# One rotary query product for two heads of a decoder step on one core

## What is computed

```python
z = x @ p['w_in'] + p['b_in']            # x: (tokens, 1024)
q = (_rms_norm(z_q, p['q_norm_g']) @ p['w_uq']).reshape(B, T, N_HEADS, QK_NOPE + QK_ROPE)   # 8 heads, 128 + 64
q_nope = q[..., :QK_NOPE]
q_rope = _apply_rope(q[..., QK_NOPE:], cos[:, None, :], sin[:, None, :])
c_kv = _rms_norm(z_kv, p['kv_norm_g'])
k_rope = _apply_rope(z_kr, cos, sin)     # one rotary key for all heads
...
def _apply_rope(x, cos, sin):
    x1, x2 = jnp.split(x, 2, axis=-1)
    return jnp.concatenate([x1 * cos - x2 * sin, x1 * sin + x2 * cos], axis=-1)
```

## Time and profile before

| | us |
|---|---|
| runs shown | 2083.44, 2084.58, 2088.0 |
| median | 2084.58 |
| profiled execution | 2083.54 |
| its span | 2081.7 |
| TensorE busy in it | 2027.8 |
| VectorE busy | 1268.9 |
| ScalarE busy | 651.7 |
| GpSimd busy | 566.2 |

### The profile page before, as it was taken

One profiled execution on the slowest core, in us unless ns is written; L12 is line 12 of the kernel. 1 busy time (PEld: TensorE's weight loads), 2 busy tenths in 40 slices (PEclk: granted clock), 3 DMA queues, 4 the chain that ended last, 5 costly groups with the idle time before them and its releaser, 6 DMA issues.

```text
span 2081.7 us, 34162 instructions
## 1 busy us (share of the span) xinstructions
PE 2027.8 (97%) x13468; PEld 1923.1 (92%) x13468; DVE 1268.9 (61%) x1746; ACT 651.7 (31%) x1099; POOL 566.2 (27%) x284
## 2 busy tenths in 40 slices
PE   8999999999999999989999999999999999999998
PEld 8999999998988888876669999999999999999997
DVE  2999999946647677655344325754545454454547
ACT  4222222225234454444342113422222222222222
POOL 4812443302110010124311245322222222222224
PEclk9999999999999999999999999999999999999999
DMA  6422233216410001145644332111111111111113
GB/s 199 158 94 76 85 105 101 80 52 213 136 58 20 16 13 43 36 166 229 242 178 145 121 113 82 31 51 51 41 51 41 51 41 51 41 51 41 51 31 128
DMA packets 164042, 182.92 MB, mean 88 GB/s; under 512 B 19917, under 2 KB 136927, under 8 KB 159821
## 3 DMA queue, kind: packets, MB, share of 16 engines
q1 hardware_dynamic: 146144, 108.68, 17.3%
q0 software_dynamic: 8320, 46.27, 5.8%
q10 hardware_dynamic: 9469, 26.36, 3.3%
HBM read 150.21 MB, written 31.93 MB: 87 GB/s over the span
## 4 chain that ended last, share of the span: by engine, by line
PE 87%; DVE 7%; issue 3%; ACT 3%; ACTq 0%; DMA 0%; POOL 0%; DVEq 0%; SPq 0%
PE psb L2124 27%; PE psa L2124 27%; PE psb L2763 6%; PE psa L2763 6%; PE psb L2313 4%; PE psa L2313 4%; PE psb L2564 1%; PE pst L2543 1%; DVE ptl L1712 1%; PE psa L2511 1%; PE psb L2511 1%; DVE nmx L1696 1%; PE pst L2386 1%; PE pst L2546 1%; PE psb L2266 1%
## 5 line engine op out<-in xcount | busy, mean ns | idle before, releaser
L1434 POOL TENSOR_TENSOR wlo<-wraw,whi 128x1024 fp32r<-128x1024 f32 x64 | 173.2, 2720 | 560.8 <-ACT whi L1226 560.8
L1536 DVE SCALAR_TENSOR_TENSOR pst<-g_ext,wtap,pst 128x512 f32<-128x512 f32 x464 | 306.9, 748 | 0.0
L1304 POOL TENSOR_TENSOR wlo<-wraw,whi 128x1024 fp32r<-128x1024 f32 x64 | 155.2, 2431 | 385.1 <-ACT whi L749 288.4
L2014 DVE TENSOR_SCALAR hg<-ueg,fwv,vec 128x1024 f32<-128x1024 f32 x22 | 20.4, 925 | 231.3 <-ACT ueg L1260 226.9
L2124 PE MATMUL psa<-x1h,whi 128*128 128x352 f32 x504 | 109.1, 324 | 0.0
L2124 PE MATMUL psb<-x1h,whi 128*128 128x352 f32 x504 | 109.0, 324 | 0.0
L2124 PE MATMUL psa<-x1h,wlo 128*128 128x352 f32 x504 | 108.6, 323 | 0.0
L2124 PE MATMUL psb<-x1h,wlo 128*128 128x352 f32 x504 | 108.6, 323 | 0.0
L2124 PE MATMUL psa<-x1l,whi 128*128 128x352 f32 x504 | 108.5, 323 | 0.0
L2124 PE MATMUL psb<-x1l,whi 128*128 128x352 f32 x504 | 108.5, 323 | 0.0
L2017 DVE SCALAR_TENSOR_TENSOR hg<-ueg,fwv,hg 128x1024 f32<-128x1024 f32 x44 | 96.9, 2203 | 5.7 <-DVE hg L2014 0.2
(11 more groups left out here) (540 smaller groups left out, 5290.5 us busy)
## 6 DMA issues: line engine op xcount, KB each, us to landing
wraw<-in_w_up SPq DMA_DIRECT2D x44, 512.0 KB, 3.7
wraw<-in_w_in SPq DMA_DIRECT2D x37, 512.0 KB, 3.8
wraw<-in_w_down SPq DMA_DIRECT2D x22, 512.0 KB, 3.6
xt_d<-tmp POOLq DMA_DIRECT2D x8, 528.0 KB, 3.4
gb_d<-stg ACTq DMA_DIRECT2D x8, 528.0 KB, 2.6
ga_d<-stg ACTq DMA_DIRECT2D x8, 528.0 KB, 3.6
ma_d<-stg ACTq DMA_DIRECT2D x8, 528.0 KB, 2.9
tmp<-gb_d SPq DMA_DIRECT2D x8, 528.0 KB, 3.8
```

The costliest lines, as they stand in the source:

```text
L1304: nc.gpsimd.tensor_tensor(wlo[:, n % HL, :], wraw[:, n % RAW, :], whi[:, n % HL, :].bitcast(F32), ALU.subtract).then_inc(lo_done, 1)
L1434: nc.gpsimd.tensor_tensor(wlo[:, (ns + 2) % HL, :], wraw[:, (ns + 2) % RAW, :], whi[:, (ns + 2) % HL, :].bitcast(F32), ALU.subtract).then_ ...
L1536: half[x] = link(nc.vector.scalar_tensor_tensor(out=dst, in0=src, scalar=tap(k_), in1=pst[:, x, :], op0=ALU.mult, op1=ALU.add))
```

## The change

1. **One rotary product for two heads.** The 128 weight columns of `pe_rope` now hold the 64 rotary columns of head 2i and the 64 of head 2i + 1, none of them swapped. It runs only at the end of odd heads (and once ahead of head 0). The loads shrink from three pieces for each head to two for each pair.
2. **Rotation out of PSUM.** For the even head VectorE reads psa crosswise: two products of 32 partitions with the halves exchanged and one of 64 (L1708, L1710 of the new code), then adds as before. The odd head's 64 partitions are copied by ScalarE in three instructions (64, 32 and 32 partitions) into a new buffer `qrb`, plain and with halves exchanged (`act_second_rope`). VectorE rotates them at the start of the even head: two products and an addition from SBUF to SBUF, around the first row maximum (`dve_second_rope`). `qrb` lies where `wukp` was loaded early, so that load now waits until the last rotation is done (`qr_t`).
3. **Even heads' ends reordered.** TensorE: key, `pe_prob` 6, `pe_out` 2, thirds 0 and 1 of the query, `pe_prob` 7, the last third, `pe_out` 3. ScalarE and VectorE follow.
4. **`pe_out` 2 and 3** start when the first group of `ptl` is made and wait for the second only at k = 4.
5. **The start.** x tiles rotate over pst, psb and two banks of psa. The first weight block is loaded second. Ten 128-column products of `ones` run ahead of the first transpose. The first third's products follow tiles 3 and 4, the second third's tiles 6 and 7.
6. **TensorE's three loops** are written out.

```diff
-        x_parts = lambda t: (psx[1][:, 0:2, :] if t % 2 else pst[:, :, :]).rearrange("p b (k n) -> p (b k) n", n=P)
+        WARM = 10
+        def x_parts(t):
+            if t == 8:
+                return psx[1][:, 2, 0:MT * NS].rearrange("p (k n) -> p k n", n=NS)
+            return (pst[:, :, :], psx[1][:, 0:2, :], psx[0][:, 1:3, :])[t % 3].rearrange("p b (k n) -> p (b k) n", n=P)
...
-                if t == 3:
+                if t == 1:
                     load(0, w_in_v[:, :, 0:P])
...
-                    for c, w, f in kr_parts:
-                        sp.dma_start(s0[:, 3:6, c:c + w], uq[:, :, bass.ds(2 * i * HQ + (s * HQ + DN + f), w)]).then_inc(hq_in, 16)
+                    if s == 0:
+                        for e in range(2):
+                            sp.dma_start(s0[:, 3:6, e * DR:(e + 1) * DR], uq[:, :, bass.ds(2 * i * HQ + (e * HQ + DN), DR)]
+                                         ).then_inc(hq_in, 16)
...
+            def act_second_rope(h):
+                act.wait_ge(proj_done, 2 * h + 1)
+                for to, p0, n in ((0, DR, DR), (DR, DR + 32, 32), (DR + 32, DR, 32)):
+                    ins = nc.scalar.activation(split(qrb[to:to + n, :]), psx[0][p0:p0 + n, :, 0:CH], ACT.Copy, scale=SCALE)
+                ins.then_inc(free[0], 2)
...
+            def dve_second_rope(h, part_):
+                if part_ == 0:
+                    dve.wait_ge(free[0], 6 * h + (U2[0] - 3))
+                    dve.wait_ge(qr_lo, h)
+                    nc.vector.tensor_tensor(qrf[0:DR, :], qrb[DR:P, :], cs[DR:P, :], ALU.mult)
+                    nc.vector.tensor_tensor(qrb[0:DR, :], qrb[0:DR, :], cs[0:DR, :], ALU.mult).then_inc(qr_t, 1)
+                else:
+                    dve.wait_ge(qr_t, 3 * h + 1)
+                    nc.vector.tensor_tensor(qrf[0:DR, :], qrf[0:DR, :], qrb[0:DR, :], ALU.add).then_inc(qr_t, 1)
+                    dve.wait_ge(qr_t, 3 * h + 2)
+                    sample_rope(h)
...
                     dve.wait_ge(proj_done, 2 * h + 1)
+                    for to, p0, t0, n in ((0, 32, DR, 32), (32, 0, DR + 32, 32)):
+                        nc.vector.scalar_tensor_tensor(out=split(qrt[to:to + n, :]), in0=psx[0][p0:p0 + n, :, 0:CH],
+                                                       scalar=SCALE, in1=split(cs[t0:t0 + n, :]), op0=ALU.mult, op1=ALU.mult)
...
                 for i in range(8):
+                    if s == 0 and i <= 1:
+                        dve_second_rope(h + 1, i)
                     dve_max(h, i)
...
+            pe.wait_ge(ones_set, 1)
+            for _ in range(WARM):
+                nc.tensor.matmul(psx[0][:, 0, 0:P], ones[:, :], ones[:, :], start=True, stop=True)
             pe.wait_ge(c_in, 16)
...
-                if t == 6:
+                if t == 3:
                     pe.wait_ge(lo_done, RAW + 1)
                     pe.wait_ge(free[0], x_tile_done(2))
                     first_third(0, range(0, 4))
+                if t == 4:
+                    first_third(0, range(4, KT))
+                if t == 6:
+                    pe.wait_ge(free[1], x_tile_done(5))
+                    pe.wait_ge(free[0], x_tile_done(4))
+                    first_third(1, range(0, 4))
                 if t == 7:
-                    first_third(0, range(4, KT))
...
             def pe_out(h, s, i2, a_):
-                pe.wait_ge(pt_lo, 12 * h + (cum(2 * a_ + 2) + 2))
+                pe.wait_ge(pt_lo, 12 * h + (cum(2 * a_ + 2) + (2 if a_ < 2 else 1)))
...
+                    if k == 4:
+                        pe.wait_ge(pt_lo, 12 * h + (cum(2 * a_ + 2) + 2))
...
+                if more and s == 0:
+                    pe_key(h + 1, 1)
+                    pe_prob(h, 6)
+                    pe_out(h, s, i2, 2)
+                    pe_query(h + 1, 1, h, (0, 1))
+                    pe_prob(h, 7)
+                    pe_query(h + 1, 1, h, (2,))
+                    pe_out(h, s, i2, 3)
+                    return
...
-            with pe.Fori(1, H // 2 - 1) as i:
+            for i in range(1, H // 2 - 1):
```

More of the change, by code:

```diff
@@ L1053, in act_head @@
                             hi_head_v(h + 1)
-                act_out(h, 2)
-                act_prob(h, 6)
-                if more:
-                    act_project(h + 1, 1 - s, "rope")
-                    act_project(h + 1, 1 - s, "query")
-                act_prob(h, 7)
-                if more:
-                    act_project(h + 1, 1 - s, "key")
-                else:
+                if more and s:
+                    act_second_rope(h + 1)
+                    act_out(h, 2)
+                    act_prob(h, 6)
+                    act_project(h + 1, 0, "rope")
+                    act_project(h + 1, 0, "query")
+                    act_prob(h, 7)
+                    act_project(h + 1, 0, "key")
+                elif more:
+                    act_project(h + 1, 1, "rope")
+                    act_project(h + 1, 1, "key")
+                    act_prob(h, 6)
+                    act_out(h, 2)
+                    act_prob(h, 7)
+                    act_project(h + 1, 1, "query")
+                else:
+                    act_out(h, 2)
+                    act_prob(h, 6)
+                    act_prob(h, 7)
                     for r in range(4):
@@ L2224, in _ @@
             last.then_inc(cl_p, 1)
-            with pe.Fori(CSUM, MT) as m:
+            for m in range(CSUM, MT):
                 in_products(m, 1)
@@ L2344, in pe_key @@
                                                  for k in range(2)])
-                last.then_inc(w_used, 1 + s)
+                last.then_inc(proj_done if s else w_used, 1 + s)
             def pe_values(h, i2, r):
@@ L2434, in pe_head @@
                 if more:
[L2435 removed]
+                    pe_query(h + 1, 0, h)
                 else:
@@ L2592, in _ @@
             pe_sample(0, 0, 0, first=True)
-            with pe.Fori(0, NB // 2 - 1) as i:
+            for i in range(0, NB // 2 - 1):
                 pe_sample(2 * i + 1, 1, i)
```

110 lines of the change are left out of this document (65 added, 45 removed).

## The result

The changed kernel takes 2069.38 us (median of 4 runs, 2067.01 to 2071.06), the kernel before 2085.56 with one more run (4 runs, 2083.44 to 2088.0). The ratio is 0.9922, 95% interval 0.991 to 0.9935. The forecast was 2070.0, between 2064.0 and 2077.5, so the time came out where it was expected. The profiled execution took 2068.43 us (span 2066.6), 15.11 less than the 2083.54 of before; 14.6 had been forecast between the two. The medians differ by more, 16.2 us, since the fourth run of the kernel before raised its median by 1.0.

The account below looks back on a forecast made before the run. TensorE was taken to bound the kernel, busy 2027.8 of 2081.7 us. Terms 17.4 + 2.0 - 1.3 - 2.0 - 1.5 + 0.5 - 0.5 gave 14.6 us gained, so 2070.0, range 2064 to 2077.5 for eight in ten.

Parts of the forecast that it names:

- even ends: Ends of even heads without the rotary product, reordered: 14.2 us instead of 18.55, four times 4.35, 17.4 gained.
- first group ahead of `pe_out`: Value products starting on the first group: 0.9 at three odd ends, 0.5 and 0.6 in head 7, 2.0 gained.
- third product ahead of head 0: VectorE's rotation out of PSUM has three products instead of two, uncovered ahead of head 0: 1.3 us lost.
- start of head 0: TensorE's wait for the first exponential grows by VectorE's two added products, 1.9, with `vl` 2.0 us lost.
- starts of heads 2, 4, 6: VectorE's 4.1 us of added rotation work mostly hidden; third value part waits 0.5, three times, 1.5 us lost.
- start: Start of the kernel up to the tables: reached at 31.9 to 33.0 instead of 33.19, 0.5 us gained.
- clock: TensorE's clock falls behind head 0's longer waits, 1.0 lost; the fall at 908 may go; net 0.5 us lost.
- loops: Writing out TensorE's loops: at most 1 us could be there by the looped heads, taken as 0.
- its cost of 0: Odd heads' ends: VectorE's third product and ScalarE's three copies cost 0, with 0.3 us to spare.
- The bound that all is exposed: Starts of heads 2, 4, 6: nothing of VectorE's added work hidden, 4.1 us each; as a rival 2080.8, chance 0.14.
- The rival from the Trainium skill's rule: At the start, x transposes lower the clock again after the warm-up products: tables at 34.9, total 2072.2 us, chance 0.12.
- the last rival: ScalarE and VectorE take turns on psa: 11.7 us more, with clock falls 18.5 lost, 2088.5 in all, chance 0.03.

Follow-up runs that it names:

- heads alone: Changed kernel with the old start and TensorE's three loops kept as loops: 2086.07 us, ratio 0.9934 to the kernel before.
- the start alone: Kernel before with only the new start (x buffers, early weight block, ten products of ones, product order): 2101.8 us, ratio 1.0005 to the kernel before.
- loops kept: Changed kernel with TensorE's three loops kept as loops instead of written out: 2071.38 us, ratio 0.9944 to the kernel before.
- The order of before: Changed kernel with even heads' ends in the old order on all three engines, rotary product still gone: 2085.49 us, ratio 1.0006 to the kernel before.
- the loops alone: Kernel before with only TensorE's three loops written out: 2100.62 us against 2100.34, ratio 1.000.
- last placement: Changed kernel with second rotation's steps ahead of the first four maxima and the output rows' DMA wait behind head 0's rotation: 2066.06 us, ratio 0.9918 to before.

## Why the prediction was right

It held in its total and in its main term, the even ends, by the mechanism that it gave. That it came within 0.6 us is partly luck: smaller terms were off by up to 1.0 each, and their errors cancelled.

| term | forecast | measured | from |
|---|---|---|---|
| even ends | +17.4 | +16.8 | 23.19 to 18.99, four times |
| first group ahead of `pe_out` | +2.0 | +2.2 beside what is in the row above | odd ends 0.44 each, head 7 0.9 |
| third product ahead of head 0 | -1.3 | -1.2, and -0.6 of a late DMA | heads alone, changed kernel |
| start of head 0 | -2.0 | -1.8 | 2.98 to 4.75 |
| starts of heads 2, 4, 6 | -1.5 | -1.0 | 0.3 each |
| start | +0.5 | +1.1, 0.4 lost again ahead of the heads | stages of one execution; not shown by the total of the start alone |
| clock | -0.5 | -1.3 | half clock behind head 0's wait; the one in head 7 stayed in this execution |
| loops | 0 | +1.0 | loops kept, 0.9 |

The forecast's terms sum to 14.6, the measured ones to 14.8, and 0.3 of the 15.11 are in none of them.

**The even ends** are right by their mechanism. The forecast's 14.2 became 14.44 because `pe_prob` 6 began at 712.50; the prediction's 712.4 is 712.25 in this execution, which reaches the stretch 0.15 earlier. The order of before shows that the 4.2 of gain in a pair stand on the reordering: the same products removed without it give nothing, of it 2.7 as the wait and the rest for the most part as lost clock. The prediction named the half microsecond that the rope product used to cover, but only for the new order; it had no number for the old one. At odd ends its cost of 0 held: they take 0.4 less than before, all of it from the first group.

**Heads' starts.** "0.5, by the nearest row" was 0.3. The bound that all is exposed (4.1 a head) was far off, but the next 1.25 were paid in full.

**Ahead of head 0** the sum was right to 0.1, though TensorE's waits fell elsewhere: 1.19 ahead of the keys and 1.06 ahead of the second value part, where one of some 2 had been expected. What the working lacked is that VectorE's start there hangs on a DMA's landing, which moves by up to 1.7 us between the traces and was late only in kernels with the new start.

**The clock.** The fall behind head 0's longer wait was forecast at 1.0 and cost about 1.3. The hope that the one behind head 7's wait would go was wrong in this execution and right in most: with the wait at 2.56, as before the change, the clock fell in four traces of four, with 2.23 in two of eight.

**The start** landed in its ranges (first product 13.44 for 12.9 to 14.0, tables 32.08 for 31.9 to 33.0), and that was partly luck: of the ten traces with this start it is one of three in which the clock did not fall behind the wait for x. In the other seven something like the rival came about, transposes at the lower clock behind the warm-up products, but behind a wait, for 3.4 us, and it was over before the first product. The rival from the Trainium skill's rule (TensorE: Matmul & The Clock Gate, section PE-mode transpose, that transposes don't count as activity) is refuted for these fp32 transposes: in three kernels the clock rose behind transposes alone. The trace before had left that open, as the prediction said, because there the clock stayed down through seven tiles and rose with the first products; what kept it down there, with waits much like those of the loops alone, is not known.

**The loops** were taken at 0 because the heads' loop showed nothing; that was extended to the sample attention's loop without reading its rows, where each pass had waits of 0.57 against 0.31 in the part outside the loop. The rows of before held this hint, and it was not used.

**Slips in the working** that changed little: 0.5 MB at 295 GB/s are 1.7 us and not 1.5; 2.5 less 0.68 is 1.8, which is what head 0 paid; the two stops at the start took 1.00 and 0.93 instead of 1.7 and 1.1; and the last rival takes off its slack once instead of at three ends (11.1 and not 11.7).

## What to carry to other kernels

When work is taken from the busiest engine, look for what that work was covering: here the same removal is worth 16.8 us or nothing, depending on what stands in its place while another engine finishes. Work added to a less busy engine is cheap up to a sharp edge, so price the next microsecond too, and look which instruction of a third engine it will meet at its new place. A wait on TensorE can cost more than itself: behind those of 3.1 us and more the clock fell each time here, and behind shorter ones sometimes.

## What was not expected of the hardware

- TensorE's clock rises behind transposes alone (1.97 us for eight, then 1.07, at 12.44), and falls again behind a wait of 2.39 for a DMA. With the old start and the new heads it fell at the same tile behind a wait of only 1.12, after two of 1.04.
- In the heads it fell behind every wait of 3.1 us and more, for 3.4 us in most cases and for 6.8 in three; behind 2.56 in four cases of four, behind 2.23 in two of eight, and behind 1.5 in head 0 in one of four. Once 2.03 was followed by a fall (last placement) and once 2.30 was not (loops kept), so the length of the wait alone does not settle it. Products of `ones` in the wait kept it up in head 0.
- A copy of 64 partitions by 32 columns, 0.36 us for two, takes 2.42 while GpSimd runs a split of 128x1024.
- On one chip the sample attention took 14 to 18 us longer than on the others, with waits ahead of the gathered pages, while the heads took the same time.
- A hardware loop on TensorE costs 0.9 us in three passes of the sample attention and nothing that can be seen in two passes of the heads.
